# A hybrid decoder layer on eight cores: the opening starts with the value projection, and the last tile's first gates move into the last attention stage

## The chip, the cores and the metric

The kernel runs on all 8 NeuronCores of one Trainium2 chip, four to a die. Each core works alone on one sequence of the batch (4096 positions of 1024 features) and there is no communication between cores. The metric is the device time of the slowest core in microseconds. The kernel before took 1575.71, 1581.21 and 1584.71 us in three runs, median 1581.21 us.

## The reference

One layer with two mixers side by side. All projections come out of one product with `w_in`.

```python
h = rms_norm(x, g_pre); proj = h @ w_in            # 1024 -> 5648
qa, ka, va, za, qb, kb, vb, zb, lr, gate_a, gate_b = split(proj)
# A: differential attention, 4 heads, two 64-wide q/k maps each, causal, ALiBi
p  = softmax(q k^T / 8 - slope * dist)             # two maps per head
oa = rms_norm((p0 - lam * p1) @ v, g_sub_a) * (1 - lam_init)
ya = (oa * silu(za)) @ w_up_a                      # 512 -> 1024
# B: gated linear attention (GLA), 4 heads, state 64 x 128, chunked
glog = log_sigmoid(lr @ w_alpha + b_alpha) / 16
ob = rms_norm(gla_chunked(qb / 8, kb, vb, glog), g_sub_b)
yb = (ob * silu(zb)) @ w_up_b
# gated merge, output projection, post norm, residual
y  = sigmoid(gate_a) * ya + sigmoid(gate_b) * yb
out = x + rms_norm(y @ w_out, g_post)
```

Inputs and outputs are float32; the kernel multiplies in bfloat16 and accumulates in float32.

## The kernel before

The 4096 positions are cut into 8 tiles of 512 (`NT`), each tile into 4 row blocks of 128. The program is one straight list of operations, written by Python loops in the order in which they are meant to run. `_Prog.emit` (L81) splits it by engine; each engine executes its own operations strictly in that order, and waits on semaphores for what it needs of the others. So an operation that waits holds up all that stands behind it on its engine.

**Weights.** They come from DRAM as float32 in pieces of 1 MB: `QA0`, `QA1`, `KA0`, `KA1` (queries and keys), `VA0`, `VA1` (values; each holds half of the contraction, so both are needed for any value row), `ZA`, `VB`, `ZB`, `QB`, gates `GA0..3`, `GB0..3`, up-projections `U0..3`, output `WO0..3`. `conv_piece` (L410) issues four 256 KB DMAs from the SP queue into 4 of 16 staging buffers, which lie in the not yet used upper halves of `KT` (buffers 0 to 7) and `V` (8 to 15), and returns a list of conversions (L379 on ScalarE, L383 on VectorE, in turn) into a slot of a ring of 7 bf16 slots (`wring`). The converted piece is also stored to a DRAM scratch (`wsc`), from which later tiles reload it (L496). The list `wseq` gives the order of all loads. `pend` holds pieces whose conversions are not yet written out; three things write them: `emit_load` (L482), which before it adds a new piece writes out the oldest until 3 are left (`flush(3)`), `acquire` (L500), which writes out all up to the piece it takes, and `tick` (L469), which at the end of each chain of matmuls writes four conversions of the next piece. `release` (L509) issues the next loads.

**Opening** (L1075 to L1111), for tiles 0 and 1 together, before the stages. `a_stat` takes the mean square of a row block (ScalarE, then a tiny step on VectorE and a power on GpSimd), `a_norm` scales it (VectorE), `a_tr` transposes it on TensorE and copies it out to `hT` (VectorE for even blocks, ScalarE for odd). Then chains of 8 matmuls, 128x512 each, make queries (`ev_q`), keys (`ev_k`) and values (`ev_v`, which scales with the table `eft`). The order is: tile 0's four blocks, queries of tile 0, keys of tile 0, with tile 1's blocks between them, queries and keys of tile 1, then values of both. A query or key chain needs all four row blocks of its tile; a value chain needs only one.

**Stages.** Stage t runs attention for tile t: 4 heads, key blocks in pairs; each pair is one step: four score matmuls (`emit_qk`), four exponentials on ScalarE (L999), 16 products with V (`emit_pv`). Five PSUM banks go round. Between those steps `pump` inserts filler from the list of `stage_units(t)`: each unit has a cost (0.26 per matmul of 512 columns), and the list is spread evenly over the stage's steps by cost. The filler of stage t is: the gate projection, merge and output projection of tile t-1 (`u_e`, `u_f`), the silu gate of tile t (`u_za`), the GLA projections of tile t, the normalisation and projections of tile t+1, and the GLA core of tile t (`core_units(k, gap, ...)`, whose k and gap scale the costs by which its short matmuls are spread). In the last stage there is no tile t+1, and the core stands alone at the end with k = 3.0, gap = 1.0.

**Tail.** After the last stage come, for tile 7, `u_e` and `u_f` alone. `u_e` has four groups p: gates (4 chains, 32 matmuls, Tanh on ScalarE at L806 into `scr`), then 4 up-projection chains of 4 matmuls (products on VectorE at L831 and L835, sum on GpSimd at L837). The first group's up-projection needs `gaT` of the last head, which comes from a chain after attention (L1037 to L1062, mostly GpSimd). `post_head` and `run_post` hold that chain.

## Time and profile before

| what | value |
|---|---|
| median of 3 runs | 1581.21 us |
| the profiled execution, its own time | 1593.94 us |
| span of its slowest core (6) | 1592.4 us |
| spans of the eight cores | 1563.1 to 1592.4 us |
| TensorE busy | 1431.3 us, 90% |
| ScalarE, VectorE, GpSimd busy | 850.7, 712.3, 476.5 us |
| moved by DMA | 207.43 MB |

The profile is of the slowest core. Busy times overlap between engines. In a timeline each line gives start, duration, engine, source line, operation, output and input tile, how many instructions are merged, and in brackets the idle time before it and what ended it. Matmuls are pipelined: a merged line of 8 matmuls that shows 1.89 us is followed by the next 1.73 us after its own start, so the step between starts is the better measure.

### The profile page before, as it was taken

The page shows a single profiled execution, that of the slowest core. Times are in us where ns is not written, and L with a number is a line of the kernel's source. Part 1 is how long each engine was busy: PE and PEld are TensorE (multiplying, and loading weights), DVE is VectorE, ACT ScalarE, POOL GpSimd, SP SyncE. Part 2 cuts the span into 40 slices and gives each one's busy share as a digit, 9 for nine tenths or more (in the row PEclk, how much of TensorE's full clock was granted, in tenths as well). Part 3 has the DMA queues.
Part 4 walks back from the last instruction along what each step waited for, and adds up shares of the span by engine and source line. Part 5 has one row for each costly group of instructions (what it writes and reads, how often), then busy time and mean ns, then how long its engine had stood idle before and what let it go on. Part 6 is the DMA issues. An engine that isn't in the chain of part 4 may idle for free.

```text
span 1592.4 us, 27810 instructions; the slowest of 8 cores (1563.1 to 1592.4 us)
## 1 busy us (share of the span) xinstructions
PE 1431.3 (90%) x10576; PEld 746.3 (47%) x10576; DVE 712.3 (45%) x1453; ACT 850.7 (53%) x1714; POOL 476.5 (30%) x469
## 2 busy tenths in 40 slices
PE   4987798999889997999989998899998999999888
PEld 2443344544344543555445554455554555544443
DVE  3558745642556334643445324453233541233434
ACT  4254355234453546355664566746667557667632
POOL 1034422433325212433214322143211350220441
PEclk9989887889999998999999999999999999999999
DMA  8789686323442225322262222622225312215022
GB/s 270 222 228 261 167 283 212 126 86 116 154 168 93 95 91 198 107 88 99 94 225 68 94 80 94 225 67 76 85 80 186 97 64 67 80 67 186 28 76 110
DMA packets 75437, 207.43 MB, mean 130 GB/s; under 512 B 7984, under 2 KB 26672, under 8 KB 75312
## 3 DMA queue, kind: packets, MB, share of 16 engines
q1 hardware_dynamic: 75312, 205.66, 39.6%
q8 instruction: 91, 1.49, 0.4%
q14 instruction: 34, 0.28, 0.1%
HBM read 173.12 MB, written 32.51 MB: 129 GB/s over the span
## 4 chain that ended last, share of the span: by engine, by line
PE 69%; DVE 12%; ACT 8%; DMA 3%; POOL 3%; issue 3%; SPq 1%; DVEq 0%; POOLq 0%
PE ps_q L270 31%; PE ps_f L270 24%; PE ps_oa L270 13%; ACT sb_PT L999 3%; DMA sb_xb<-x 2%; DVE sb_scr L872 1%; DVE sb_scr L893 1%; ACT sb_junk L890 1%; DVE sb_wring L383 1%; ACT sb_ztmp L638 1%; DVE sb_rz L1025 1%; ACT sb_hb L589 1%; DVE sb_tmpo L1027 1%; DMA sb_V<-w_in 1%; DMA sb_KT<-w_in 1%
## 5 line engine op out<-in xcount | busy, mean ns | idle before, releaser
L999 ACT ACTIVATE sb_PT<-ps_q 128x512 bf16<-128x512 f32 (+3 forms) x697 | 359.8, 564 | 250.2 <-PE ps_q L270 153.9
L270 PE MATMUL ps_oa<-sb_V,sb_PT 128*128 128x129 bf16 x4224 | 345.7, 222 | 10.8 <-ACT sb_PT L999 4.9
L270 PEld LDWEIGHTS ps_oa<-sb_V,sb_PT 128*128 128x128 bf16 x4224 | 286.6, 99 | 139.9 <-issue 37.3
L999 ACT ACTIVATE sb_PT<-ps_f 128x512 bf16<-128x512 f32 (+3 forms) x455 | 247.0, 569 | 148.8 <-PE ps_f L270 84.8
L270 PE MATMUL ps_q<-sb_hT,sb_wring 128*128 128x512 bf16 x1048 | 265.2, 389 | 7.6 <-ACT sb_wring L379 3.8
L837 POOL TENSOR_TENSOR sb_yT<-sb_scr 128x512 bf16<-128x512 f32 x64 | 81.6, 1278 | 395.5 <-DVE sb_scr L835 395.3
L270 PE MATMUL ps_f<-sb_hT,sb_wring 128*128 128x512 bf16 x744 | 188.1, 386 | 5.6 <-DVE sb_qtT L698 1.6
L270 PE MATMUL ps_q<-sb_QT,sb_KT 64*128 64x512 bf16 (+3 forms) x697 | 155.8, 364 | 22.5 <-DVE sb_vb L688 9.3
L270 PE MATMUL ps_q<-sb_wring,sb_hT 128*128 128x512 bf16 x584 | 154.8, 402 | 14.3 <-ACT sb_PT L999 5.1
L270 PEld LDWEIGHTS ps_q<-sb_hT,sb_wring 128*128 128x128 bf16 x1048 | 95.4, 99 | 126.1 <-issue 51.3
L270 PE MATMUL ps_f<-sb_QT,sb_KT 64*128 64x512 bf16 (+3 forms) x455 | 128.4, 369 | 9.8 <-DVE sb_gaT L1062 3.8
L270 PE MATMUL ps_f<-sb_wring,sb_hT 128*128 128x512 bf16 x440 | 121.0, 414 | 11.6 <-DVE sb_yT L639 2.8
L270 PEld LDWEIGHTS ps_f<-sb_hT,sb_wring 128*128 128x128 bf16 x744 | 67.4, 99 | 85.5 <-issue 32.5
L1037 POOL TENSOR_TENSOR sb_oaf<-sb_tmpo 128x512 f32<-128x512 f32 x32 | 40.6, 1268 | 193.8 <-DVE sb_tmpo L1027 193.8
L270 PEld LDWEIGHTS ps_q<-sb_wring,sb_hT 128*128 128x128 bf16 x584 | 54.5, 102 | 81.1 <-issue 44.5
L806 ACT ACTIVATE sb_scr<-ps_q 128x512 f32<-128x512 f32 x76 | 46.1, 606 | 65.8 <-PE ps_q L270 65.4
L270 PE MATMUL ps_q<-sb_wring,sb_yT 128*128 128x512 bf16 x288 | 73.7, 394 | 6.1 <-DVE sb_rz L1024 2.2
L831 DVE SCALAR_TENSOR_TENSOR sb_scr<-sb_scr,ps_q 128x512 f32<-128x512 f32 x40 | 27.4, 687 | 103.3 <-PE ps_q L270 103.1
L270 PEld LDWEIGHTS ps_f<-sb_wring,sb_hT 128*128 128x128 bf16 x440 | 41.9, 104 | 66.3 <-issue 39.2
L593 POOL TENSOR_TENSOR sb_rstd<-sb_rs,sb_lams 128x1 f32<-128x1 f32 x32 | 17.6, 551 | 173.5 <-DVE sb_rs L591 173.5
L772 POOL TENSOR_TENSOR sb_rstdb<-sb_rsb,sb_lams 128x4 f32<-128x4 f32 x32 | 32.3, 1009 | 118.6 <-DVE sb_rsb L770 118.6
L270 PE MATMUL ps_f<-sb_wring,sb_yT 128*128 128x512 bf16 x224 | 57.4, 385 | 7.0 <-DVE sb_scr L893 2.8
(177 smaller groups left out, 1864.2 us busy)
## 6 DMA issues: line engine op xcount, KB each, us to landing
sb_wring<-wsc SPq DMA_DIRECT2D x204, 512.0 KB, 3.8
sb_xb<-x SPq DMA_DIRECT2D x60, 512.0 KB, 5.8
out<-sb_scr SPq DMA_DIRECT2D x32, 512.0 KB, 3.4
wsc<-sb_wring SPq DMA_DIRECT2D x30, 512.0 KB, 9.6
sb_KT<-w_in SPq DMA_DIRECT2D x48, 256.0 KB, 9.1
sb_V<-w_in SPq DMA_DIRECT2D x40, 256.0 KB, 8.7
...
```

The costliest lines, as they stand in the source:

```text
L270: P.op("pe", lambda e: e.matmul(out=out_, lhsT=lhsT, rhs=rhs, start=start, stop=stop, **kw), reads=reads, writes=writes)
L383: dve(lambda e: e.tensor_scalar(out=dst_ap, in0=src_ap, scalar1=scale_ap, scalar2=scale_c, op0=ALU.mult, op1=ALU.mult), rd, [key])
L589: act(lambda e: e.activation(out=scrap, in_=ap, func=AF.Square, accum_out=ss[:, g:g + 1]), keys, skeys + [f"ss{g}"])
L593: pool(lambda e: e.tensor_tensor(out=rstd[:, g:g + 1], in0=rs[:, g:g + 1], in1=lams[:, 5:6], op=ALU.pow), [f"rs{g}", "nhalf"], [f"rstd{g}"])
L638: act(lambda e: e.activation(out=ztmp[:], in_=BANK[b][:, :], func=AF.Tanh, scale=0.5), [b], ["ztmp"])
L772: pool(lambda e: e.tensor_tensor(out=rstdb[:, sl], in0=rsb[:, sl], in1=lams[:, 5:6].to_broadcast([128, 4]), op=ALU.pow), [f"rsb{s}", "nhal ...
L806: act(lambda e: e.activation(out=dst, in_=BANK[b][:, :], func=AF.Tanh, scale=0.5), [b], [key])
L831: dve(lambda e: e.scalar_tensor_tensor(out=ta[j], in0=ta[j], scalar=1.0, in1=BANK[b][:, :], op0=ALU.add, op1=ALU.mult), [b, f"s{j}"], [f"s ...
L837: pool(lambda e: e.tensor_tensor(out=yT[:, jj, :], in0=ta[j], in1=tb[j], op=ALU.add), [f"s{j}", f"s{2 + j}"], [f"yT{jj}"])
L872: dve(lambda e, hh=hh: e.scalar_tensor_tensor(out=zg[hh], in0=zg[hh], scalar=rstdz[:, g:g + 1], in1=ap[:, hh * 512:(hh + 1) * 512], op0=AL ...
L999: act(lambda e, pp=pp, m=m, c0=c0, b=b, cbias=cbias: e.activation(out=PT[pp][:, m, c0:512], in_=BANK[b][:, c0:512], func=AF.Exp, bias=cbia ...
L1037: pool(lambda e: e.tensor_tensor(out=oaf[:], in0=v4[:, :, 0, :], in1=v4[:, :, 1, :], op=ALU.add), ["tmpo0", "tmpo1", "tmpo2"], ["oaf"])
```

## The change

In the opening, the load order becomes `VA0, VA1, QA0, QA1, KA0, KA1`, with row blocks of x between, and `eft` comes with the first constants. The value rows of tile 0 are computed block by block, as each block is normalised; then queries of tile 0, mixed with blocks and value rows of tile 1; queries of tile 1; and keys of both. `tick` writes out no conversions until the value rows of tile 0 are written (`ahead`). The up-projection weights' constant factors are folded into two columns computed once, so that half of their conversions can go to ScalarE. In the last stage, the first gate group of tile 7 is merged into the core's units, whose k and gap become 1.5 and 0.5, and the tail orders its groups so that gates run one group ahead, with a second set of four gate buffers in the unused `hT` of tile 6.

```diff
         x_load()
-        consts("sp", "cstA", [(ident[:], ident_d, "ident"), (smalls[:], smalls_d, "smalls")])
-        xst["limit"] = 4
-        x_load()
+        consts("sp", "cstA", [(ident[:], ident_d, "ident"), (smalls[:], smalls_d, "smalls"), (eft[:], ef_d, "eft")])
...
+            for c_, f_ in ((0, (1.0 - LAM_INIT) * 0.5), (1, 0.5)):
+                dve(lambda e, c_=c_, f_=f_: e.tensor_scalar(out=lams[:, 6 + c_:7 + c_], in0=smalls[:, 8 + c_:9 + c_], scalar1=f_, scalar2=None,
+                                                            op0=ALU.mult), ["smalls"], ["upsc"])
...
-                for n, (src, sc, c_) in enumerate(((w_up_a, smalls[:, 8:9], (1.0 - LAM_INIT) * 0.5), (w_up_b, smalls[:, 9:10], 0.5))):
+                for n, (src, sc, c_) in enumerate(((w_up_a, lams[:, 6:7], 1.0), (w_up_b, lams[:, 7:8], 1.0))):
...
         SEQ_G = ["VB0", "VB1", "ZB0", "ZB1", "QB0", "QB1"]
-        wseq = QKV + SEQ_Z + SEQ_G
+        wseq = QKV[4:6] + QKV[0:4] + SEQ_Z + SEQ_G
         for t in range(1, ntiles):
             wseq = wseq + SEQ_E0 + SEQ_Z + SEQ_E + SEQ_G + (QKV if t + 1 < ntiles else [])
-        wseq = wseq + SEQ_E0 + SEQ_E
+        wseq = wseq + SEQ_E0 + ["GA1", "GB1", "U0", "GA2", "GB2", "U1", "GA3", "GB3", "U2", "U3"] + [f"WO{i}" for i in range(4)]
         wst = {"loaded": 0, "acq": 0, "seen": set()}
         pend = []
 
...
         calm = [False]
+        ahead = [False]
 
         def tick():
-            if pend and pend[0][0] <= wst["acq"]:
+            if pend and pend[0][0] <= wst["acq"] and ahead[0]:
                 for _ in range(4):
                     if pend[0][1]:
                         pend[0][1].pop(0)()
...
-            ta = [scr[:, 0, :], scr[:, 1, :]]
-            tb = [scr[:, 2, :], scr[:, 3, :]]
+            last = t + 1 == ntiles
+            hf = hT[(t + 1) % 2][:].rearrange("p a b -> p (a b)").bitcast(F32).rearrange("p (a b) -> p a b", a=4)
+            order = []
             for p_ in range(4):
                 st = {}
                 gates = []
+                units = []
+                order.append((gates, units))
+                own = last and p_ % 2 == 0
+                src = hf if own else scr
+                ta = [src[:, 0, :], src[:, 1, :]]
+                tb = [src[:, 2, :], src[:, 3, :]]
+                gk = [f"g{n}" if own else f"s{n}" for n in range(4)]
                 for j in range(2):
-                    for nm, dst, key in (("a", ta[j], f"s{j}"), ("b", tb[j], f"s{2 + j}")):
-                        def ev(b, dst=dst, key=key):
-                            act(lambda e: e.activation(out=dst, in_=BANK[b][:, :], func=AF.Tanh, scale=0.5), [b], [key])
+                    for nm, dst, key in (("a", ta[j], gk[j]), ("b", tb[j], gk[2 + j])):
+                        def ev(b, dst=dst, key=key, more=hkeys(t + 1) if own and p_ == 0 else []):
+                            act(lambda e: e.activation(out=dst, in_=BANK[b][:, :], func=AF.Tanh, scale=0.5), [b], [key] + more)
                         u = fm_chain(t, lambda st=st, nm=nm: st[nm], j, ev)
                         if j == 0:
                             u = before(u, lambda st=st, nm=nm, p_=p_: st.update({nm: acquire(("GA" if nm == "a" else "GB") + str(p_))}))
                         gates += u
-                gates = then(gates, lambda: release(2))
-                if p_ == 0:
-                    head = gates
-                else:
-                    units += gates
+                gates[:] = then(gates, lambda: release(2))
                 ups = [[], []]
                 for j in range(2):
                     jj = 2 * p_ + j
...
                     ups[1] += ub
                 units += ups[0] + ups[1] if p_ == 0 else ups[0][0:1] + ups[1][0:1] + ups[0][1:] + ups[1][1:]
-            return head, units
+            (h0, u0), (h1, u1), (h2, u2), (h3, u3) = order
+            if last:
+                return h0, h1 + u0 + h2 + u1 + h3 + u2 + u3
+            return h0, u0 + h1 + u1 + h2 + u2 + h3 + u3
 
         posts = []
 
...
             if t + 1 == ntiles:
-                units = units + core_units(3.0, 1.0, True)
+                units = units + merge(core_units(1.5, 0.5, True), last_e[0])
             elif t >= 1:
...
+                kk = k % 4
+                mm(BANK[b][:, :], hT[t % 2][:, k, s * 128:(s + 1) * 128], wring[:, sl, kk * 512:(kk + 1) * 512], st_, sp_,
+                   [f"w{sl}_{kk}", f"hT{t % 2}_{s}"], [b])
+            run_units(chain(8, one, lambda b: ev_v(t, s, b)))
...
-            return res
-
+        xlim(4)
         emit_load()
-        pst["QA0"] = acquire("QA0")
+        xlim(6)
         emit_load()
-        pst["QA1"] = acquire("QA1")
-        two = ntiles > 1
-        a1 = a_units(1) if two else []
-        run_units(merge(pro_fm(0, "QA", ev_q), a1[0:5]))
+        xlim(8)
+        a_stat(0, 0)
+        a_norm(0, 0)
         emit_load()
-        pst["KA0"] = acquire("KA0")
         emit_load()
-        pst["KA1"] = acquire("KA1")
         consts("sp", "cstB", [(ztmp[:], w_alr, "ztmp"), (lamv_st, lamv_d, "oaf"), (tri[:], tri_d, "tri"), (negm[:], negm_d, "negm"),
-                              (eft[:], ef_d, "eft"), (rmask[:], rmask_d, "rmask")])
-        run_units(merge(pro_fm(0, "KA", ev_k), a1[5:]))
+                              (rmask[:], rmask_d, "rmask")])
         emit_load()
-        if two:
-            run_units(pro_fm(1, "QA", ev_q))
+        take("VA0")
+        a_tr(0, 0)
+        take("VA1")
+        v_row(0, 0)
+        a_stat(0, 1)
+        a_norm(0, 1)
+        a_stat(0, 2)
+        a_tr(0, 1)
+        a_norm(0, 2)
+        v_row(0, 1)
+        a_stat(0, 3)
+        a_tr(0, 2)
+        a_norm(0, 3)
+        v_row(0, 2)
+        a_tr(0, 3)
+        v_row(0, 3)
+        take("QA0")
+        ahead[0] = True
+        q00 = pro_fm(0, "QA0", ev_q)
+        run_units(q00[0:2])
+        a_stat(1, 0)
+        run_units(q00[2:])
+        a_norm(1, 0)
+        a_stat(1, 1)
+        a_tr(1, 0)
+        a_norm(1, 1)
+        take("QA1")
+        q01 = pro_fm(0, "QA1", ev_q)
+        run_units(q01[0:2])
+        a_tr(1, 1)
+        v_row(1, 0)
+        a_stat(1, 2)
+        run_units(q01[2:])
+        a_norm(1, 2)
+        v_row(1, 1)
+        a_stat(1, 3)
+        a_tr(1, 2)
+        a_norm(1, 3)
+        v_row(1, 2)
+        a_tr(1, 3)
+        v_row(1, 3)
         release(2)
-        if two:
-            run_units(pro_fm(1, "KA", ev_k))
+        run_units(pro_fm(1, "QA0", ev_q) + pro_fm(1, "QA1", ev_q))
         release(2)
         setup_small()
-        run_units(tm_chunk([0, 1] if two else [0], QKV[4:6], ev_v))
+        take("KA0", "KA1")
+        run_units(pro_fm(0, "KA0", ev_k) + pro_fm(0, "KA1", ev_k) + pro_fm(1, "KA0", ev_k) + pro_fm(1, "KA1", ev_k))
+        release(2)
 
         calm[0] = True
         prev = []
+        last_e = u_e(ntiles - 1)
         for t in range(ntiles):
             if t == 3:
                 ones_col(1)
...
         emit_pv(*prev[1])
-        head, body = u_e(ntiles - 1)
-        tail = head[0:4] + [w(0.4, g_tr, 3)] + head[4:] + body + u_f(ntiles - 1)
+        body = last_e[1]
+        tail = body[0:4] + [w(0.4, g_tr, 3)] + body[4:] + u_f(ntiles - 1)
         for _, f, _ in tail:
```

The up-projection's evictions take the buffers chosen above (`ga_`, `gb_`) instead of `ta[j]`, `tb[j]`; nothing else in them changes.

## Rows read from the trace of the kernel before

**Rows 1.** The page, part 2: the span in 40 slices, PE's busy tenths.
```profile
PE   4987798999889997999989998899998999999888
```

**Rows 2.** Windows of the opening: length, busy of PE, PEld, DVE, ACT, POOL, PEclk, DMA share, GB/s.
```profile
0.00:5.00 5.00, 0.00 (x0) 0.00 (x0) 0.00 (x0) 1.96 (x2) 2.59 (x9) 1.00 0.44 135
5.00:10.00 5.00, 1.01 (x8) 0.77 (x8) 0.91 (x2) 1.14 (x3) 0.55 (x1) 1.00 0.86 252
10.00:15.00 5.00, 1.77 (x16) 1.55 (x16) 2.41 (x5) 3.35 (x6) 1.10 (x2) 1.00 0.96 285
15.00:20.00 5.00, 1.56 (x12) 0.91 (x10) 3.40 (x10) 2.20 (x6) 0.55 (x1) 1.00 0.95 292
20.00:25.00 5.00, 5.00 (x18) 1.95 (x17) 1.17 (x3) 2.35 (x6) 0.00 (x0) 1.00 0.99 348
30.00:35.00 5.00, 2.77 (x13) 1.57 (x14) 3.30 (x9) 2.06 (x6) 1.10 (x2) 0.50 0.95 262
```

**Rows 3.** Timeline of PE in the opening.
```profile
19.71 3.47 PE L270 MATMUL ps_q<-sb_hT,sb_wring 128*128 128x512 bf16 x8 [1.60 <-ACT sb_wring L379]
23.01 3.62 PE L270 MATMUL ps_f<-sb_hT,sb_wring 128*128 128x512 bf16 x16
...
32.23 1.01 PE L610 MATMUL ps_q<-sb_ident,sb_hb 128*128 128x128 bf16 x8 [4.74 <-DVE sb_hb L601]
...
74.98 1.03 PE L270 MATMUL ps_q<-sb_wring,sb_hT 128*128 128x512 bf16 x4
```

**Rows 4.** Timeline of DVE in the opening.
```profile
5.50 0.15 DVE L591 TENSOR_SCALAR sb_rs<-sb_ss 128x1 f32<-128x1 f32 x1 [5.50 <-ACT sb_PT L589]
6.32 0.76 DVE L601 TENSOR_SCALAR sb_hb<-sb_xb,sb_rstd 128x1024 bf16<-128x1024 f32 x1 [0.67 <-POOL sb_rstd L593]
10.59 0.68 DVE L614 COPY sb_hT<-ps_f 128x1024 bf16<-128x1024 bf16 x1
20.48 0.35 DVE L383 TENSOR_SCALAR sb_wring<-sb_KT,sb_smalls 128x256 bf16<-128x256 f32 x1 [0.36 <-DMA sb_KT<-w_in]
70.00 0.69 DVE L628 TENSOR_TENSOR sb_V<-ps_q,sb_eft 128x512 bf16<-128x512 f32 x1 [1.03 <-PE ps_q L270]
```

**Rows 5.** Timeline of ACT in the opening.
```profile
28.57 0.51 ACT L379 ACTIVATE sb_wring<-sb_V,sb_smalls 128x256 bf16<-128x256 f32 x1 [0.22 <-DVE sb_wring L383]
45.62 1.02 ACT L616 ACTIVATE sb_hT<-ps_f 128x1024 bf16<-128x1024 bf16 x1 [2.83 <-PE ps_f L610]
```

**Rows 6.** Timeline of DVE in stage 1: conversions of up-projection pieces.
```profile
177.00 3.05 DVE L383 TENSOR_SCALAR sb_wring<-sb_V,sb_smalls 128x512 bf16<-128x512 f32 x4
212.16 2.68 DVE L383 TENSOR_SCALAR sb_wring<-sb_KT,sb_smalls 128x512 bf16<-128x512 f32 x4
```

**Rows 7.** Timeline of PE in the last stage: score matmuls of successive steps.
```profile
1449.39 0.39 PE L270 MATMUL ps_f<-sb_QT,sb_KT 64*128 64x512 bf16 x1
1452.68 0.39 PE L270 MATMUL ps_f<-sb_QT,sb_KT 64*128 64x512 bf16 x1
...
1507.61 0.39 PE L270 MATMUL ps_q<-sb_QT,sb_KT 64*128 64x512 bf16 x1
1510.56 0.39 PE L270 MATMUL ps_q<-sb_QT,sb_KT 64*128 64x512 bf16 x1
```

**Rows 8.** Timeline of PE in the tail.
```profile
1524.34 1.89 PE L270 MATMUL ps_q<-sb_hT,sb_wring 128*128 128x512 bf16 x8
...
1534.10 0.38 PE L1060 MATMUL ps_q<-sb_ident,sb_gtA 128*128 128x128 bf16 x4 [2.48 <-POOL sb_gtA L1053]
...
1539.54 1.89 PE L270 MATMUL ps_q<-sb_hT,sb_wring 128*128 128x512 bf16 x8
1541.27 1.89 PE L270 MATMUL ps_f<-sb_hT,sb_wring 128*128 128x512 bf16 x8
```

**Rows 9.** Timeline of POOL at the end of the last stage.
```profile
1527.20 1.26 POOL L1037 TENSOR_TENSOR sb_oaf<-sb_tmpo 128x512 f32<-128x512 f32 x1
```

**Rows 10.** Timeline of ACT in the tail.
```profile
1526.26 0.60 ACT L806 ACTIVATE sb_scr<-ps_q 128x512 f32<-128x512 f32 x1 [2.30 <-PE ps_q L270]
```

More of the change, by code:

```diff
@@ L373, in conv @@
         def conv(dst_ap, src_ap, stg, key, scale_ap, scale_c):
-            rd = [f"stg{stg}"] + (["smalls"] if scale_ap is not None else [])
+            rd = [f"stg{stg}"] + (["smalls", "upsc"] if scale_ap is not None else [])
             cctr[0] += 1
@@ L1073, in run_units, with take, xlim, pro_fm @@
                 f()
+        pst = {}
+        def take(*names):
+            for nm in names:
+                pst[nm] = acquire(nm)
+        def xlim(n):
+            xst["limit"] = n
+            x_load()
+        def pro_fm(t, nm, ev):
+            res = []
+            for jj in range(2):
+                res += fm_chain(t, lambda: pst[nm], jj, lambda b, jj=jj: ev(t, 2 * int(nm[2]) + jj, b))
+            return res
+        def v_row(t, s):
+            def one(b, k, st_, sp_):
+                sl = pst[f"VA{k // 4}"]
+                kk = k % 4
+                mm(BANK[b][:, :], hT[t % 2][:, k, s * 128:(s + 1) * 128], wring[:, sl, kk * 512:(kk + 1) * 512], st_, sp_,
+                   [f"w{sl}_{kk}", f"hT{t % 2}_{s}"], [b])
+            run_units(chain(8, one, lambda b: ev_v(t, s, b)))
```

26 lines of the change are left out of this document (7 added, 19 removed).

## The prediction

> **What bounds the kernel now.** I read the slices first. PE shows 8 or 9 tenths nearly everywhere, except in the first slice (4) and in slices 4, 5 and the last stretch [rows 1]. So TensorE sets the pace, and time is to be had where it sits idle: in the opening, and where attention's own loop leaves it free. Then the opening by windows and by timeline. The DMA engines run at 0.86 to 0.99 from 5 us on, at 252 to 348 GB/s [rows 2], and TensorE starts its first projection at 19.71 us, waits 4.74 us for tile 1's first block at 32.23, and starts the last stretch of the opening's work so late that stage 0's first matmul stands at 74.98 [rows 3]. The opening has 192 matmuls of 512 columns; at the 0.216 us of the full clock (8 in 1.73 us, the step from 1539.54 to 1541.27 [rows 8]) they are 41.5 us. Some 33 of the 75 us are waiting, transposes and low clock. Then the end. In the last 13 or so steps of stage 7, where only the GLA core is filler, a step takes 2.95 us; where 8 filler matmuls stand in a step it takes 3.29 [rows 7]. So 8 matmuls, worth 1.73 us alone, cost 0.34 us as filler there. In the tail, four chains run from 1524.34, then TensorE waits 2.48 us for the last head's normalised output (to 1534.10), and from there it is busy without a break worth naming [rows 8].
>
> **The opening: when the first value row can start.** What the diff puts into the SP queue before the first query piece's last byte: x block 0, VA0, VA1, x blocks 1 to 3, QA0. That is 4 x 0.524 + 3 x 1.049 + 0.04 (constants) = 5.28 MB. Adding the windows up (5 us each): 0.67, 1.93, 3.36, 4.82 MB at 5, 10, 15, 20 us, then 348 GB/s [rows 2], so 5.28 MB is reached at 21.3 us. Landing lags that sum: before, QA1's last bytes are number 4.24 MB (18.0 us by the sum), and the conversion that waits for them starts at 20.48 [rows 4], 2.5 us later. So QA0 has landed at 23.8 us; with the larger rows of the value pieces perhaps at 22.5.
>
> Why QA0 matters to a value row: conversions are written into the engines' lists by the order of calls. Between `a_norm(0, 0)` and `take("VA0")` there are three `emit_load`s of new pieces (KA0, KA1, ZA0) with four pieces pending, and each writes out the oldest: VA0, VA1 and, with ZA0, QA0. So QA0's eight conversions stand on VectorE and ScalarE ahead of the copy of the first block into `hT` (VectorE) and ahead of `a_stat(0, 1)` (ScalarE). Both engines wait there for QA0's bytes, though VA1 (2.66 MB) has landed at about 12.5 + 2.5 = 15 us. This is the step on which most of my forecast rests. After QA0's last conversion (0.51 [rows 5]) and the copy (0.68 [rows 4]) the first row starts at 23.8 + 0.5 + 0.7 = 25.0 us; I take 24, with the faster DMA.
>
> **The opening: the rows of tile 0.** First row: 8 matmuls at the low clock. Before, the first 8 took 3.3 us from 19.71 to 23.01, the next 16 a step of 3.46 [rows 3]: 27.5. Then a chain across engines, because block 1's statistics stand behind the first row's eviction on VectorE: eviction 0.69 [rows 4], statistics to normalisation 0.82 (5.50 to 6.32), normalisation 0.76 [rows 4], transposes 1.01 (low) [rows 3], copy on ScalarE 1.02 [rows 5], two hand-overs of 0.15: 4.5 us, the second row starts at 32.0. The third and fourth rows have their blocks normalised meanwhile, and wait for transposes and copy: 0.6 + 0.7 + 0.15 and 0.6 + 1.02 + 0.15, plus an eviction's rest: 1.6 and 1.8 us. With the second row at the low clock (3.4) and the others at the full one (1.73): 32.0 + 3.4 + 1.6 + 1.7 + 1.8 + 1.7 = 42.2 us. Bounds: all at the full clock from the second row on and short hand-overs 39.5, all at the low clock 46.
>
> Of the clock, the row shows 0.50, the lower of the two levels (1.2 GHz), in 30 to 35 us, after TensorE had idled 4.74 us [rows 2, 3]; the new rows leave gaps of 1.6 to 4.5 us between bursts of 1.7 to 3.4. The Trainium skill, "TensorE: Matmul & The Clock Gate", section "HAM oscillation — how this bites in real kernels", speaks against such an order: bursts shorter than the wait for the next data start cold each time. By it the value rows would all be slow; the 0.50 agrees with it; the mechanism is rival B, priced there from rows.
>
> **The opening: the rest.** 160 matmuls (32 queries of tile 0, 32 values of tile 1, 32 queries of tile 1, 64 keys) x 0.216 = 34.6 us; four blocks of transposes x 0.45 = 1.8. Waits: `a_norm(1, 0)` stands behind the eviction of the second query chain and two conversions on VectorE (0.69 + 0.6 + 0.76 + 0.15 = 2.2 us), the third and fourth row of tile 1 wait for their copies (1.1 and 1.15): 4.5 us. Keys: KA1's last byte is 5.2 MB behind QA0's, at 262 to 348 GB/s [rows 2] some 18 us later, about 42 us, and the keys start at about 42 + 27 = 69, so DMA hides. `setup_small` (some 3 us on VectorE) is hidden by five free banks, as it was ahead of the values. Sum 40.9 us; the opening ends at 42.2 + 40.9 = 83.1 against 74.98: **+8 us**, between +3 and +13. The ring then stands as before (three pieces ahead converted or landed), as the releases come in the same order and at the same distance from the opening's end; so stage 0 gives nothing back.
>
> **Constants and conversions of the up-projection.** Two tiny VectorE steps (0.15 each) more in `setup_small`, hidden. Of 16 conversions on VectorE 8 move to ScalarE. Four of one piece took 3.05 and 2.68 us [rows 6] in a stretch where ScalarE has room. VectorE is spared 4 x 1.4 = 5.5 us in stage 1; a part of it was on the path: between 0 and -4, I take **-2**.
>
> **Last stage.** Costs by L946 to L955 and the 0.26 per matmul: the filler before the core is 101.4; the core was 26.8 and becomes 13.4, the gates add 8.3: 128.2 becomes 123.1 over 64 steps. So 2.00 per step becomes 1.92, the core's stretch shrinks from 13.4 steps to 11.3, and the filler before it is spread over 52.7 steps in place of 50.6. Of those, 46.9 held 8 matmuls and 3.7 held 4; now 44.8 and 7.9: 46.9 x 3.29 + 3.7 x 2.95 = 165.2 us, now 170.7: +5.5. The core's stretch: 13.4 x 2.95 = 39.5, now 11.3 x 3.05 (2.8 gate matmuls a step are under what is free, a Tanh of 0.60 us [rows 10] in four of them): 34.5, so -5. Together **+0.5**, between -3 and +4. Nothing of the gates shows in the stage; what hides them is the attention loop's own wait.
>
> **Tail.** The first four chains stay, only that they are now group 1's gates; they cover the same wait to 1534.10. After it there are 32 matmuls fewer: -6.9 us. GpSimd had the core's last two products to 1527.2 ahead of the last head's sum (starts at 1527.20 [rows 9]); the smaller gap lets them come a part of a step sooner: 0 to -0.7. The last two groups' up-projections stand together: 8 chains of 0.86 us with a VectorE step of 0.69 each, as for other evictions of this size [rows 4], so it keeps up. WO3's load follows group 3's gates, 6.9 us ahead of its use. **-7.2**.
>
> **Sum.** +8 - 2 + 0.5 - 7.2 = -0.7 against the execution's 1593.94. That one is 12.7 us above the median of 1581.21, so I forecast 1580.5 for the median.
>
> **Rivals.** *A, the opening does not wait for QA0* (the conversions are written later than I read it, or the engines pass them by): first row at 15 + 0.5 + 0.7 = 16, rows paced by x blocks, which land from 17 us on, tile 0's rows done at 34; 34 + 40.9 = 75, opening 0; with fewer waits, as more work is at hand, -3. Sum -9 to -12, 1570. For it speaks that VA1 is there at 15 us; against it the order of the calls. *B, slower: the rows keep TensorE at 1.2 GHz.* If all 64 value matmuls of both tiles step at 0.43 us, they cost 13.8 us more than at full clock, of which 3.4 are counted: +10, sum +9.7, 1591. It decides if the last value row still takes 3.4 us. For it speaks the 0.50 in 30 to 35 [rows 2]; against it, that after 3.3 us of unbroken matmuls the next 16 went at full speed [rows 3], and that in tile 1 query chains stand between the rows. *C, the gates are not hidden:* the stage is bound by TensorE in more steps than I count, and 32 matmuls cost there what they cost in the tail. Sum +6.3, 1587.5; against it the 2.95 us step with its idle time.
>
> **Chances.** Forecast 0.45, A 0.27, B 0.17, C 0.11. What a measurement can tell is 0.5%, 7.9 us: faster means under 1573.3, slower over 1589.1. Faster: most of A and the edge of the forecast (opening +3, stage -3), 0.29. Slower: most of B and parts of C and the forecast, 0.25. Same 0.46. The range 1568 to 1592 holds A's middle and B's; my forecast alone would be 1573 to 1588.
>
> **What would show it.** In the timeline of PE, the first value chain at 23 to 26 us, not at 16; ahead of it on VectorE and ScalarE QA0's conversions, waiting for DMA. Four chains of 8 with gaps till 40 to 46 us. Stage 0's first matmul at 80 to 86. In the last stage, Tanh (L806) of tile 7 among the last steps, at a step of about 3.0 us, and in the tail after the wait 6.9 us less. The prediction is wrong if the opening ends before 77 us or after 90, or if the last stage ends more than 4 us off.

## The result, and the profile after

The changed kernel takes 1590.34 us (median of 10 runs) against 1580.39 us before: ratio 1.0064, 95% interval 1.0048 to 1.0079. It is 10 us slower. I had forecast 0.7 us less, with a chance of 0.46 for no change and 0.25 for slower.

Where it went is read best by stage. The table gives, as the median over the eight cores, the time from the program's start to the first exponential of stage 0 (the opening), then from the first exponential of each stage to that of the next, then from the start of the last exponential to the end (the tail). All come from the timelines of ScalarE.

```
us                   opening  st.0  st.1   st.2   st.3   st.4   st.5   st.6   st.7   tail
before                  77.7  58.5 184.9  166.9  182.9  191.1  202.6  220.5  217.2   68.7
changed kernel          91.4  59.1 184.2  170.3  183.1  190.6  202.9  220.4  223.3   59.0
changed opening alone   91.7  59.1 189.4  170.1  182.7  190.9  203.8  220.5  217.2   68.7
changed end alone       77.7  57.7 189.5  169.8  182.6  191.1  203.8  220.5  222.6   59.0
```

Opening +13.7, last stage +6.1, tail -9.7: together +10.1, the measured loss. Stage 1 differs by up to 13 us from core to core in one execution too (181.6 to 194.5 before), and stages 1 and 2 move without direction over the kernels of this study, so nothing is made of them.

The opening first. Timeline of PE of the changed kernel's slowest core (0); it answers [rows 3].

```profile
7.99 1.01 PE L612 MATMUL ps_f<-sb_ident,sb_hb 128*128 128x128 bf16 x8 [7.99 <-DVE sb_hb L603]
25.50 3.37 PE L270 MATMUL ps_f<-sb_wring,sb_hT 128*128 128x512 bf16 x8 [16.50 <-DVE sb_hT L616]
31.21 0.61 PE L612 MATMUL ps_q<-sb_ident,sb_hb 128*128 128x128 bf16 x8 [2.34 <-DVE sb_rs L593]
33.02 3.57 PE L270 MATMUL ps_q<-sb_wring,sb_hT 128*128 128x512 bf16 x8 [1.21 <-ACT sb_hT L618]
...
38.32 3.57 PE L270 MATMUL ps_f<-sb_wring,sb_hT 128*128 128x512 bf16 x8 [0.88 <-DVE sb_hT L616]
...
43.74 1.89 PE L270 MATMUL ps_q<-sb_wring,sb_hT 128*128 128x512 bf16 x8 [1.21 <-ACT sb_hT L618]
45.47 3.62 PE L270 MATMUL ps_q<-sb_hT,sb_wring 128*128 128x512 bf16 x16
52.44 1.01 PE L612 MATMUL ps_f<-sb_ident,sb_hb 128*128 128x128 bf16 x8 [3.36 <-DVE sb_hb L603]
53.25 3.17 PE L270 MATMUL ps_f<-sb_hT,sb_wring 128*128 128x512 bf16 x8
...
90.77 1.03 PE L270 MATMUL ps_q<-sb_wring,sb_hT 128*128 128x512 bf16 x4
```

TensorE stands for 16.50 us before the first value row. Rows 1, 2 and 3 take 3.4 us each, the fourth 1.73. That is this core: the third row is slow on cores 0 and 7 alone and takes 1.73 us on the other six, as in the forecast. Over the eight cores the first row starts at 24.35 us at the median, the first query chain at 43.2 (41.5 to 45.5), and stage 0's first matmul stands at 88.6. Stage 0's first matmul, at 74.98 before [rows 3], stands at 90.77. What the first row waited for is in the timeline of DVE of the same core, answering [rows 4]:

```profile
14.99 0.49 DVE L384 TENSOR_SCALAR sb_wring<-sb_KT,sb_smalls 128x512 bf16<-128x512 f32 x1 [1.99 <-DMA sb_KT<-w_in]
21.36 0.35 DVE L384 TENSOR_SCALAR sb_wring<-sb_V,sb_smalls 128x256 bf16<-128x256 f32 x1 [5.88 <-DMA sb_V<-w_in]
24.40 0.35 DVE L384 TENSOR_SCALAR sb_wring<-sb_V,sb_smalls 128x256 bf16<-128x256 f32 x1 [0.43 <-DMA sb_V<-w_in]
24.67 0.68 DVE L616 COPY sb_hT<-ps_f 128x1024 bf16<-128x1024 bf16 x1
...
50.36 0.15 DVE L593 TENSOR_SCALAR sb_rs<-sb_ss 128x1 f32<-128x1 f32 x1 [1.75 <-ACT sb_PT L591]
```

VA1 (in `KT`) is in at 14.99. VectorE then waits 5.88 us for QA0's first bytes (in `V`), and only behind QA0's last conversion copies block 0 into `hT`. The transposes had been ready since 9.0 us.

The windows of the same core, answering [rows 2], show the granted clock in the seventh column of numbers: its lower level (0.50, 1.2 GHz) again after the waits. The column does not show it for the first row (1.00 in 25 to 30 us, where eight matmuls take 3.4 us); there the step between matmuls is what tells.

```profile
30.00:35.00 5.00, 2.59 (x13) 1.20 (x14) 1.57 (x3) 2.06 (x3) 0.82 (x2) 0.69 0.99 308
35.00:40.00 5.00, 4.12 (x17) 1.84 (x16) 2.10 (x4) 0.00 (x0) 0.54 (x1) 0.50 1.00 290
40.00:45.00 5.00, 3.79 (x19) 1.85 (x18) 0.69 (x1) 1.02 (x1) 0.00 (x0) 0.78 0.99 312
50.00:55.00 5.00, 2.56 (x13) 1.49 (x14) 3.50 (x8) 2.27 (x6) 1.08 (x2) 0.74 0.70 222
```

Now the tail, timeline of PE of the changed kernel; it answers [rows 8].

```profile
1530.75 1.89 PE L270 MATMUL ps_f<-sb_hT,sb_wring 128*128 128x512 bf16 x8
...
1539.44 0.38 PE L1066 MATMUL ps_f<-sb_ident,sb_gtA 128*128 128x128 bf16 x4 [1.40 <-POOL sb_gtA L1059]
1539.67 1.14 PE L270 MATMUL ps_q<-sb_gaT,sb_wring 128*128 128x512 bf16 x4
1540.65 1.02 PE L270 MATMUL ps_f<-sb_gaT,sb_wring 128*128 128x512 bf16 x4
```

From the tail's first gate chain to the last head's transposes it is 8.69 us, before 9.76 [rows 8]: 1.1 us less. And behind the wait the 4-matmul chains run at full speed, 0.98 and 0.86 us apart. In the kernel before they were slow there, as the windows of both show, before first (core 6), then changed:

```profile
1535.00:1540.00 5.00, 5.00 (x17) 1.88 (x17) 2.33 (x4) 0.00 (x0) 0.35 (x1) 0.66 0.05 18
```

```profile
1540.00:1545.00 5.00, 5.00 (x25) 2.11 (x23) 3.04 (x5) 0.00 (x0) 1.66 (x2) 1.00 0.32 105
```

After 2.48 us of idle time [rows 8] the granted clock was 0.66 in that window; after 1.40 us it stayed at 1.00. But the length of the wait does not decide it. In the same execution of the kernel before, all eight cores idle 2.46 to 2.48 us at this place; six are granted 0.66 in the 5 us behind it, and cores 3 and 7 are granted 1.00. Core 3:

```profile
1516.64:1521.64 5.00, 5.00 (x26) 2.31 (x27) 3.17 (x5) 0.00 (x0) 1.10 (x1) 1.00 0.09 34
```

From the last exponential's end those two have tails of 66.8 and 67.1 us, the others 68.4 to 69.4: the low clock costs about 1.6 us there. In the changed kernel GpSimd was free for the last head's sum when its inputs came (answers [rows 9]):

```profile
1532.47 1.26 POOL L1043 TENSOR_TENSOR sb_oaf<-sb_tmpo 128x512 f32<-128x512 f32 x1 [2.24 <-DVE sb_tmpo L1033]
```

### The profile page after: what moved, and what is told of

Read it like the earlier page. It is cut to its first block, busy times and chain, and to the rows that moved or that the text cites. A ratio compares the mean times of both kernels' runs of the same rounds, so it can differ in the third digit from the quotient of the medians.

```text
span 1589.2 us, 27796 instructions; the slowest of 8 cores (1577.4 to 1589.2 us)
## 1 busy us (share of the span) xinstructions
PE 1410.8 (89%) x10576; PEld 740.8 (47%) x10576; DVE 708.3 (45%) x1447; ACT 856.6 (54%) x1722; POOL 476.7 (30%) x469
## 4 chain that ended last, share of the span: by engine, by line
PE 69%; DVE 13%; ACT 9%; POOL 3%; issue 3%; DMA 3%; SPq 1%; DVEq 0%; POOLq 0%
PE ps_q L270 32%; PE ps_f L270 22%; PE ps_oa L270 12%; ACT sb_PT L1005 3%; DMA sb_xb<-x 2%; DVE sb_scr L899 2%; DVE sb_scr L878 1%; ACT sb_junk L896 1%; ACT sb_ztmp L640 1%; ACT sb_hb L591 1%; DVE sb_rz L1031 1%; DVE sb_wring L384 1%; DMA sb_V<-w_in 1%; DVE sb_tmpo L1033 1%; DVE sb_qtT L700 1%
## 5 line engine op out<-in xcount | busy, mean ns | idle before, releaser
L1005 ACT ACTIVATE sb_PT<-ps_q 128x512 bf16<-128x512 f32 (+3 forms) x685 | 351.4, 563 | 238.6 <-PE ps_q L270 156.3
L270 PE MATMUL ps_q<-sb_hT,sb_wring 128*128 128x512 bf16 x1104 | 271.1, 380 | 8.6 <-ACT sb_wring L380 2.2
L841 POOL TENSOR_TENSOR sb_yT<-sb_scr 128x512 bf16<-128x512 f32 x60 | 76.6, 1279 | 370.1 <-DVE sb_scr L839 353.4
L270 PE MATMUL ps_q<-sb_wring,sb_hT 128*128 128x512 bf16 x616 | 161.4, 398 | 19.9 <-ACT sb_PT L1005 5.4
L270 PE MATMUL ps_f<-sb_hT,sb_wring 128*128 128x512 bf16 x688 | 170.8, 382 | 2.2 <-ACT sb_wring L380 0.9
L270 PE MATMUL ps_f<-sb_wring,sb_hT 128*128 128x512 bf16 x408 | 111.8, 412 | 27.7 <-DVE sb_hT L616 17.4
L270 PE MATMUL ps_f<-sb_QT,sb_KT 64*128 64x512 bf16 (+3 forms) x467 | 126.8, 368 | 10.3 <-DVE sb_gaT L1068 3.5
L270 PEld LDWEIGHTS ps_f<-sb_hT,sb_wring 128*128 128x128 bf16 x688 | 61.7, 98 | 74.7 <-issue 18.2
L270 PE MATMUL ps_q<-sb_wring,sb_yT 128*128 128x512 bf16 x304 | 79.5, 400 | 6.8 <-DVE sb_rsz L910 2.5
L814 ACT ACTIVATE sb_scr<-ps_q 128x512 f32<-128x512 f32 x75 | 45.4, 605 | 56.2 <-PE ps_q L270 55.7
L835 DVE SCALAR_TENSOR_TENSOR sb_scr<-sb_scr,ps_f 128x512 f32<-128x512 f32 x24 | 16.5, 688 | 110.5 <-PE ps_f L270 110.5
L774 POOL TENSOR_TENSOR sb_rstdb<-sb_rsb,sb_lams 128x4 f32<-128x4 f32 x32 | 32.3, 1009 | 110.7 <-DVE sb_rsb L772 110.7
L914 POOL TENSOR_TENSOR sb_rstdz<-sb_rsz,sb_lams 128x1 f32<-128x1 f32 x32 | 27.2, 851 | 124.9 <-DVE sb_rsz L912 105.9
```

The lines of the kernel that those rows point to most:

```text
L270: P.op("pe", lambda e: e.matmul(out=out_, lhsT=lhsT, rhs=rhs, start=start, stop=stop, **kw), reads=reads, writes=writes)
L774: pool(lambda e: e.tensor_tensor(out=rstdb[:, sl], in0=rsb[:, sl], in1=lams[:, 5:6].to_broadcast([128, 4]), op=ALU.pow), [f"rsb{s}", "nhal ...
L814: act(lambda e: e.activation(out=dst, in_=BANK[b][:, :], func=AF.Tanh, scale=0.5), [b], [key] + more)
L835: dve(lambda e: e.scalar_tensor_tensor(out=ga_, in0=ga_, scalar=1.0, in1=BANK[b][:, :], op0=ALU.add, op1=ALU.mult), [b, ka_], [ka_])
L841: pool(lambda e: e.tensor_tensor(out=yT[:, jj, :], in0=ga_, in1=gb_, op=ALU.add), [ka_, kb_], [f"yT{jj}"])
L914: pool(lambda e: e.tensor_tensor(out=rstdz[:, g:g + 1], in0=rsz[:, g:g + 1], in1=lams[:, 5:6], op=ALU.pow), [f"rsz{g}", "nhalf"], [f"rstdz ...
```

## The experiments

Each is compared with the kernel before, run beside it. All stage lengths are medians over cores, as in the table above. A shown edit is the step from the kernel it is nearest to: the changed kernel, or the run that the text names.

**The changed opening alone.** Last stage, tail and conversions are those of before. From the changed kernel:

```diff
-            units = units + merge(core_units(1.5, 0.5, True), last_e[0])
+            units = units + core_units(3.0, 1.0, True)
...
```

> The changed opening alone; last stage, tail and conversions as before. Theory (the parts add up): the opening ends some 14 us later, as in the changed kernel (median over cores of the first exponential: 91.4 against 77.7 us), nothing gives it back, so +13 to +14 us on the whole. Rival (a late start is partly given back in stages 0 to 2, because the weight pieces are then further ahead): +6 to +9 us, and the stages 0 to 2 shorter than before by the rest.

Ratio 1.0089 (1.0055 to 1.0124), +14 us. The opening is 91.7 us, 14.0 more, and no later stage is more than 0.2 us shorter than before. The late start is not given back.

**The changed last stage and tail alone.** From the changed kernel:

```diff
-        wseq = QKV[4:6] + QKV[0:4] + SEQ_Z + SEQ_G
+        wseq = QKV + SEQ_Z + SEQ_G
...
```

> The changed last stage and tail alone; opening and conversions as before. Theory: the last stage is 6 us longer and the tail 9.7 us shorter, as in the profile of the changed kernel, so -3.5 us. Rival (the stage's +6 comes from the later start or the other conversions, or from one core's clock): stage within 2 us of before, whole -8 us.

Ratio 0.9968 (0.9942 to 0.9993), -5 us with an interval from -9 to -1; by stages 222.6 and 59.0, so -4.3. The stage's +5.4 is there without the late start and without the other conversions. The rival is out by the stage, though not by the whole time. The 0.7 us to the changed kernel's +6.1 is low clock: see the part on the last stage below.

**The wait for QA0 taken away.** The opening alone, with ZA0 loaded after `take("QA0")`.

```diff
-        emit_load()
         take("VA0")
...
         take("QA0")
+        emit_load()
```

> As e_open_only, but the load of ZA0 stands behind take(QA0), so QA0's conversions no longer stand ahead of the first value row on VectorE and ScalarE. Theory (the wait for QA0's bytes delays all rows): first row at 17 to 18 us in place of 25.5, opening ends 8 us earlier than in e_open_only, whole +5 to +6 against before. Rival (the chain from row to row and the later x blocks set the pace): first row early, but the opening ends only 2 to 3 us earlier than in e_open_only, whole +11.

Ratio 1.0035 (1.0002 to 1.0067), +5.5 us; opening 84.5 in place of 91.7. Timeline of PE (core 5):

```profile
15.20 3.17 PE L270 MATMUL ps_f<-sb_wring,sb_hT 128*128 128x512 bf16 x8 [6.05 <-DVE sb_hT L613]
20.72 0.61 PE L609 MATMUL ps_q<-sb_ident,sb_hb 128*128 128x128 bf16 x8 [2.35 <-DVE sb_rs L590]
22.53 3.57 PE L270 MATMUL ps_q<-sb_wring,sb_hT 128*128 128x512 bf16 x8 [1.21 <-ACT sb_hT L615]
...
36.72 3.61 PE L270 MATMUL ps_q<-sb_hT,sb_wring 128*128 128x512 bf16 x16 [1.68 <-ACT sb_wring L377]
```

The first row starts 10.3 us sooner than on the core shown above (9.4 at the median over cores), even before the 17 to 18 I had written, and the opening ends 7.2 us sooner. A new wait of 1.68 us for QA0's conversions at 36.72 is the only thing that moving them cost on this path. One line in the order of loads is half of the opening's loss. With it away, the opening is still 6.8 us longer than before.

**Block 1's normalisation ahead of the first row's eviction.**

```diff
         take("VA1")
-        v_row(0, 0)
         a_stat(0, 1)
         a_norm(0, 1)
+        v_row(0, 0)
```

> As e_open_nowait, and block 1's statistics and normalisation stand ahead of the first row's eviction. Theory (after the wait, the round trip row, eviction, statistics, normalisation, transposes is next): second row 2 us sooner than in e_open_nowait, opening 2 us shorter, whole +3 to +4. Rival (TensorE's lower clock level in short bursts is what costs): rows still step at 0.43 us a matmul, and the gain is under 1 us.

Ratio 1.0016 (0.9989 to 1.0044), opening 82.2: 2.3 us less than the run before. Timelines of PE and DVE (core 7):

```profile
15.52 3.57 PE L270 MATMUL ps_f<-sb_wring,sb_hT 128*128 128x512 bf16 x8 [6.16 <-DVE sb_hT L613]
19.88 1.01 PE L609 MATMUL ps_q<-sb_ident,sb_hb 128*128 128x128 bf16 x8 [0.80 <-DVE sb_hb L600]
22.10 3.57 PE L270 MATMUL ps_q<-sb_wring,sb_hT 128*128 128x512 bf16 x8 [1.21 <-ACT sb_hT L615]
...
36.47 3.61 PE L270 MATMUL ps_q<-sb_hT,sb_wring 128*128 128x512 bf16 x16 [1.68 <-ACT sb_wring L377]
```

```profile
18.17 0.15 DVE L590 TENSOR_SCALAR sb_rs<-sb_ss 128x1 f32<-128x1 f32 x1 [2.79 <-ACT sb_PT L588]
```

On this core, the slowest, the second row comes only 0.4 us sooner than on the one shown for the run before: block 1's statistics wait 2.79 us for ScalarE, which had to wait for the block's bytes. Over the eight cores the second row starts at 21.3 us at the median, before at 23.0: 1.7 us sooner, near the 2 of the theory. In these two openings the cores differ more than the medians do (80.1 to 85.2 us here, 82.6 to 85.7 in the run before), so the size of the 2.3 us is not settled by a single execution.

**The clock kept up.** As the last, with 39 matmuls read by nobody in the waits.

```diff
+        def dummy(n):
+            b = falloc()
+            for _ in range(n):
+                mm(BANK[b][:, :], ident[:, :], qtT[:, 0, 0, :], True, True, ["ident", "qtT0"], [b])
...
+        dummy(20)
         v_row(0, 0)
+        dummy(8)
...
+        dummy(4)
         v_row(0, 1)
```

and 3 and 4 of them ahead of the third and fourth row.

> As e_open_pipe, with 39 matmuls of 512 columns (identity times zeros, read by nobody) in the waits before the value rows of tile 0. Theory (the low clock level costs 1.6 us in each of three rows): rows at 0.216 us a matmul, opening 4 to 5 us shorter than in e_open_pipe (82.2), whole -1 to -2 against before. Rival (the rows wait for x blocks, transposes and copies; speed inside a row is hidden): opening at most 1 us shorter.

Ratio 1.0036 (1.0023 to 1.0049). Timeline of PE (core 0):

```profile
8.72 6.40 PE L270 MATMUL ps_f<-sb_qtT,sb_ident 128*128 128x512 bf16 x20
15.46 1.89 PE L270 MATMUL ps_q<-sb_wring,sb_hT 128*128 128x512 bf16 x8 [0.33 <-DVE sb_hT L613]
...
21.88 1.89 PE L270 MATMUL ps_f<-sb_wring,sb_hT 128*128 128x512 bf16 x8 [0.34 <-ACT sb_hT L615]
...
28.84 1.89 PE L270 MATMUL ps_q<-sb_wring,sb_hT 128*128 128x512 bf16 x8 [0.34 <-ACT sb_hT L615]
32.40 3.61 PE L270 MATMUL ps_q<-sb_hT,sb_wring 128*128 128x512 bf16 x16 [1.68 <-ACT sb_wring L377]
```

All rows take 1.73 us now, on every core. Against the core shown for the run before, the query chain starts 4.1 us sooner (32.40 against 36.47), but that core is the only one of the eight where the third row was slow. At the median over cores the second row starts no sooner (21.7 against 21.3 us), the query chain 0.7 us sooner (32.3 against 33.0), and the opening is 80.5 us, 1.7 less. So my theory was wrong and the rival nearly right: most of what a fast row gains is lost again in the waits for blocks, transposes and copies. The slowest core of each execution shows 81.0 against 85.2, and the spread between cores 1.2 against 5.1 us. The whole time did not show the gain: the run before measured 1.0016 and this one 1.0036, with overlapping intervals. My -1 to -2 for the whole was wrong, and why not even the 1.7 us shows stays open.

**Transposes one block ahead.** As e_open_pipe with another order of calls.

```diff
         a_tr(0, 1)
         a_norm(0, 2)
-        v_row(0, 1)
         a_stat(0, 3)
         a_tr(0, 2)
         a_norm(0, 3)
-        v_row(0, 2)
+        v_row(0, 1)
         a_tr(0, 3)
+        v_row(0, 2)
+        a_stat(1, 0)
+        a_norm(1, 0)
         v_row(0, 3)
...
+        a_stat(1, 1)
         run_units(q00[0:2])
-        a_stat(1, 0)
-        run_units(q00[2:])
-        a_norm(1, 0)
-        a_stat(1, 1)
         a_tr(1, 0)
         a_norm(1, 1)
+        a_stat(1, 2)
+        run_units(q00[2:])
...
```

> As e_open_pipe, with transposes one block ahead of the rows and tile 1's statistics ahead of the query chains. Theory (round trips between engines in a list written in strict order are what is left): tile 0's rows done at 31 to 33 us (36.5 in e_open_pipe), no wait of 3.4 us at tile 1's first block, opening ends at 68 to 71 in place of 75.0 before, whole -4 to -6. Rival (the pace is set by DMA landing and the low clock): opening 76 to 78, whole 0.

Ratio 0.9977 (0.9964 to 0.9989), -3.6 us; opening 75.0. Timeline of PE (core 6):

```profile
23.34 3.62 PE L270 MATMUL ps_q<-sb_wring,sb_hT 128*128 128x512 bf16 x8
...
29.11 1.89 PE L270 MATMUL ps_q<-sb_wring,sb_hT 128*128 128x512 bf16 x8
33.03 2.70 PE L270 MATMUL ps_q<-sb_hT,sb_wring 128*128 128x512 bf16 x8 [2.03 <-ACT sb_wring L377]
35.52 1.06 PE L609 MATMUL ps_q<-sb_ident,sb_hb 128*128 128x128 bf16 x8
...
72.82 1.03 PE L270 MATMUL ps_q<-sb_wring,sb_hT 128*128 128x512 bf16 x4
```

Tile 0's rows are done at 30.8 us (29.11 + 1.73), and no wait stands ahead of tile 1's first transposes at 35.52, where the changed kernel has 3.36. The same projections in the value-first order now beat the old opening, by 2.7 us. I had written 68 to 71 for its end; it is 72.8 on this core and 72.3 at the median. A wait for QA0's conversions (2.03) and low clock remain.

**Both first gate groups ahead of the tail's first up-projection.** Nothing is moved into the last stage. From e_last_only:

```diff
-        body = last_e[1]
+        body = last_e[0] + last_e[1]
```

with the core alone in the stage, at k = 3.0, gap = 1.0.

> Opening, conversions and last stage (core alone, k = 3.0, gap = 1.0) as before; only the tail changes: both first gate groups of tile 7 (64 matmuls) stand ahead of the first up-projection, and the groups then run one ahead. Theory (the tail's second gain is the wait for the last head and the low clock behind it, not the gates moved): 13.8 us of gate matmuls cover the wait, so 2.5 us of idle time and 1.7 us of low clock go, tail 64.5 in place of 68.7 us, stage 217.2 as before, whole -4. Rival (only moving gates out of the tail shortens it): tail 68 or more, whole 0.

Ratio 0.9981 (0.9969 to 0.9993), -3.0 us; stage 217.2, tail 64.3 (-4.4). Timeline of PE (core 0):

```profile
1518.32 1.89 PE L270 MATMUL ps_f<-sb_hT,sb_wring 128*128 128x512 bf16 x8
1520.05 0.39 PE L1064 MATMUL ps_q<-sb_ident,sb_gtA 128*128 128x128 bf16 x4
1520.27 1.89 PE L270 MATMUL ps_f<-sb_hT,sb_wring 128*128 128x512 bf16 x8
```

The last head's transposes (L1064) stand between gate chains without a wait. The 2.5 us of idle time and some 1.6 us of low clock make 4.1 of the 4.4.

**The core's costs kept, the gates merged in.** From e_last_only:

```diff
-                units = units + merge(core_units(1.5, 0.5, True), last_e[0])
+                units = units + merge(core_units(3.0, 1.0, True), last_e[0])
```

> As e_last_only, but the core's costs stay at k = 3.0, gap = 1.0 while the gates are merged in. Theory (the stage pays because 2 more steps stand in front, and because dense core units wait for each other): front as before or 4 us shorter (179.4 before, 184.6 in e_last_only), back some 46 to 49 us, stage 222 to 225 as in e_last_only, so its +6 is nearly the moved work itself in either spreading, whole -4 to -6. Rival (the spreading alone is at fault and the gates are free): stage 218 or less, whole -9.

Ratio 0.9971 (0.9955 to 0.9987); stage 222.0, tail 59.0. Up to the core's first transposes (L717, L715) the stage takes 173.5 us (179.4 before, 184.6 in e_last_only), from there 48.5 (37.8 and 38.0). The first part I call the front, the second the back. The sum is the same to within 0.6 us of e_last_only.

**The core's costs halved, no gates.**

```diff
-                units = units + core_units(3.0, 1.0, True)
+                units = units + core_units(1.5, 0.5, True)
```

> The kernel before, with the core's costs at k = 1.5, gap = 0.5 and nothing merged into it. By the costs the core's stretch falls from 12.8 to about 7 steps and the front grows by 6. Theory (what one stretch gives up the other pays: a step costs about 2.6 us wherever it stands): front 195, back 21 to 23, stage 216 to 219. Rival (dense core units wait for each other and for PSUM banks, and that is what held the back at 38 us in the changed kernel): back 26 or more, stage 221 or more.

Ratio 1.0014 (0.9991 to 1.0036); front 196.8, back 25.5, stage 222.5. Neither theory is right. The back shrank nearly as the costs say, but the front grew by 17.4 us for 6 steps. The stage is 5.3 us longer with none of the gates in it. That is no price of the thinner spacing as such: the 17th step of the stage takes 13.0 to 13.3 us on the eight cores, where it took 5.0. Timeline of PE (core 0):

```profile
1351.09 0.58 PE L1060 MATMUL ps_q<-sb_ident,sb_gtA 128*128 128x128 bf16 x4 [7.29 <-POOL sb_gtA L1053]
1351.47 1.91 PE L270 MATMUL ps_q<-sb_gaT,sb_wring 128*128 128x512 bf16 x4
```

By the order of the calls, L842 writes out what is left of a head's chain ahead of an up-projection group. With the filler thinner, such a group falls right behind the first head's end, so the head's transposes stand at once behind its five GpSimd steps; the matmuls behind them run at the low clock. Without that one step the stage would be some 3 us shorter than before (my estimate, 222.5 - 8.1 against 217.2; no run takes it away). The tail of this run is 67.5 us, 1.2 less than before.

**The conversions of the up-projection alone.** From the kernel before; the two columns are computed as in the change.

```diff
-    ((w_up_a, smalls[:, 8:9], (1.0 - LAM_INIT) * 0.5), (w_up_b, smalls[:, 9:10], 0.5))
+    ((w_up_a, lams[:, 6:7], 1.0), (w_up_b, lams[:, 7:8], 1.0))
```

> Only the up-projection's conversions changed, half of the 16 on ScalarE. Theory (part of VectorE's 5.5 us was on the path of stage 1): stage 1 shorter by 1 to 3 us. Rival (VectorE's backlog there is hidden, or ScalarE's later exponentials give it back): stage 1 within 0.7 us, whole unchanged.

Ratio 1.0006 (0.9974 to 1.0038); stage 1 is 183.8, 1.1 us less. Not to be told from nothing, as stage 1 differs more than that between the cores of this run (180.1 to 184.7).

**Together.** The opening of e_open_best, the last stage of e_last_k3, the changed conversions. From the changed kernel:

```diff
-                units = units + merge(core_units(1.5, 0.5, True), last_e[0])
+                units = units + merge(core_units(3.0, 1.0, True), last_e[0])
...
-        v_row(0, 0)
         a_stat(0, 1)
         a_norm(0, 1)
+        v_row(0, 0)
...
```

> Everything that gained, together: the opening of e_open_best, the last stage of e_last_k3 with its tail, and the changed conversions. Theory (the parts add up): opening -2.7, last stage and tail -4.8, conversions 0 to -1 (from the stage lengths of the runs so far), whole -7 to -8.5. Rival (they share a gain, or a shorter opening is lost in the weight loads of stages 0 and 1): -4 or less.

Ratio 0.9943 (0.9928 to 0.9958), 9 us less than the kernel before. Opening 74.9 (-2.8), stage 222.1 (+4.9), tail 59.0 (-9.7): -7.6 by the parts, inside the interval of -7 to -11. The parts add up.

## Why the prediction was wrong

**The start of the rows: right.** I followed the order of the calls to QA0's conversions and put the first row at 25.0 us by the sum, then took 24; it is at 25.50 on the slowest core and 24.35 at the median. (QA0's last bytes were there at 24.4 on that core; the 22.5 that I had allowed for did not come.) e_open_nowait shows the cause: 9.4 us at the first row at the median, 7.2 at the opening's end. Rival A is out.

**The rows: right, but for the slowest core.** The round trip between first and second row came as worked out (7.52 us from start to start; I had 8.0). I let only two rows run at the low clock, and on six of eight cores only two did. On the slowest core three did (3.37, 3.57, 3.57), so tile 0 was done at 45.47, not 42.2: 1.5 us from the start, the rest from the third row. At the median it was done at 43.2. Rival B, all rows at the low clock, is wrong for the third row on six cores, for the fourth on all, and for tile 1, where all value rows of the shown core took 1.73. Its total of +9.7 is near the measured +10.1 by luck: it had +18 for the opening. The Trainium skill, "TensorE: Matmul & The Clock Gate", section "HAM oscillation — how this bites in real kernels", tells of a kernel whose bursts, shorter than the waits for data, start cold each time. The rows here do not settle it: bursts of 3.4 us ran at the low clock (0.50 in 35 to 40 us) behind waits of only 0.9 to 2.3 us, and others behind such waits ran at full speed.

**The rest of the opening: too cheap by 4.4 us, the failed step.** The prediction's waits of 4.5 us and its "Sum 40.9 us" measured 45.3 (90.77 - 45.47; 45.4 between the medians). This is most of the error of the opening, which came out beyond the stated bounds (+13.7 against +3 to +13). I had queued `a_norm(1, 0)` behind VectorE's work alone. ScalarE does two conversions of QA1, then the mean square of tile 1's first block, which ends at 50.3 us; the tiny step behind it on VectorE waits 1.75 us for it, until 50.36, and stands ahead of a query eviction, two conversions and the normalisation. TensorE waits 3.36 us instead of 2.2, falls to the low clock and pays 3.0 us for the next 8 matmuls instead of 1.73, and a wait of 1.26 us, which I had not counted at all, comes once more at the third block. These three make 3.7 of the 4.4 us. e_open_best, which writes these statistics and normalisations earlier, has no wait there, and its opening is 7.2 us shorter than that of e_open_pipe; it moves tile 0's transposes too, so the two are not told apart.

**The last stage: the failed step.** "The core's stretch ... now 11.3 x 3.05 ...: 34.5, so -5. Together +0.5." The front grew by 5.9 us (I had +5.5, by luck in part: I had priced it at 165.2 us, and it took 179.4). The back did not shrink: 38.0 against 37.8. Divided by the steps that my own costs give, the runs tell what each change does to a step of the back:

| back | steps | us | us a step |
|---|---|---|---|
| before | 13.4 | 37.8 | 2.82 |
| gates, old spacing (e_last_k3) | 16.5 | 48.5 | 2.94 |
| no gates, spacing halved (e_k15_nogate) | 7.5 | 25.5 | 3.41 |
| gates, spacing halved (changed kernel) | 11.3 | 38.0 | 3.36 |

The gates add 0.12 us to a step, and I had 0.10: that was right. The halved spacing of the core's units adds 0.4 to 0.6 us to a step, with or without gates, and I had put it at nothing. That is 3.5 us (11.3 x 0.31) of the 5.6 by which the stage was mis-sized; another 1.7 is that 13.4 steps before cost 37.8 us and not my 39.5. In the changed kernel's timeline of PE a score matmul and a core matmul wait for VectorE there:

```profile
1503.02 0.37 PE L270 MATMUL ps_f<-sb_QT,sb_KT 64*128 64x512 bf16 x1 [0.74 <-DVE sb_ATs L727]
1520.73 0.22 PE L270 MATMUL ps_f<-sb_vb,sb_ATs 128*128 128x128 bf16 x1 [0.55 <-DVE sb_ATs L727]
```

More tells in the windows of the back, before (core 6), then changed (core 1):

```profile
1485.90:1523.70 37.80, 31.22 (x343) 18.02 (x340) 16.02 (x32) 25.89 (x54) 15.47 (x17) 1.00 0.01 3
1482.20:1520.20 38.00, 31.96 (x335) 19.15 (x334) 16.84 (x33) 24.02 (x49) 18.72 (x19) 1.00 0.09 29
```

TensorE was busy 31.2 of the 37.8 us before and 32.0 of 38.0 after: about half a microsecond idle in a step both times (its busy time is modelled, so tenths count for little). My 34.5 us would have left it 2.5 us in 11.3 steps. Over the whole stage, on these cores, TensorE's busy time rose by 4.9 us (196.4 to 201.3) and its idle time by 0.4. Nor does the other spacing avoid it: in e_last_k3 the steps of the back are cheap, but there are three more of them, and the stage is 222.0. So rival C, that the stage is bound by TensorE in more steps than I counted, is right in size (+6.1 for the 6.9 moved) and nearer to the reason than my forecast. That e_k15_nogate is as long (222.5) without gates does not speak against it: its excess stands in one step of 13.1 us that no other kernel has.

One more wait is in the changed kernel's front. The second head's transposes (L1066) wait 2.71 us on all eight cores, where before they waited 0.2; e_last_only has it too. On cores 0, 2, 5 and 6 the granted clock falls behind it (0.50 to 0.69 in the next 5 us), and their stage takes 224.1 to 225.5 us; on the other four it stays at 1.00 and the stage takes 222.5. That is the +6.1 against +5.4.

**The tail: right in its main term, 2.5 us too small.** 6.9 us of gate work gone, 1.1 us because GpSimd is free for the last head's sum (I had 0 to 0.7), and a low clock of some 1.6 us behind the wait that I had not seen in my own row, though the chains after it were there to read. The 1.1 us do not come from the smaller gap, as I had it: e_last_k3 keeps the old gap and has the same tail of 59.0, and e_k15_nogate has the smaller one and its last head's transposes wait 2.87 us, longer than before. They come with the merged gates. e_tail_ahead covers the wait and the low clock with gates instead.

**The conversions: a size.** -2 against -1.1 in stage 1 of e_up_only, inside the bounds of 0 to -4, and not to be seen in the whole.

The sum: +8 became +13.7, +0.5 became +6.1, -7.2 became -9.7, -2 became about 0. The stated range held the time; the sign and the likeliest case were wrong, and both signs of error that the prediction named came true on the profiled core (stage 0's first matmul at 90.77, after 90, though 88.6 at the median; the last stage 5.6 us off). That the range held is luck: my forecast alone was 1573 to 1588, and 1590.34 is inside only because the range was widened to hold the middle of rival B, which is not what happened. The two largest errors went the same way: in the opening I had counted waits of short work by one engine only, and in the last stage I had counted on idle time that TensorE did not have.
